# Gate and up projections in token-major form, and a Fourier token transform that sums in four pair banks

## The chip, the cores and the metric

The kernel runs on one core of a Trainium2 chip. The metric is the device time of one execution in microseconds (us), from the kernel's start to its end; the lower the better.

## What is computed

Two transformer blocks on 256 tokens of width 1024, in float32. The parts that matter here:

```
ff = silu(h @ w_gate) * (h @ w_up) @ w_down          # hidden width 2816, three times in all
f  = fftn(h.reshape(B, S, 4, 256), axes=(1, 3), norm="ortho").real
m  = f.reshape(B, S, 1024) @ w_fourier_out           # the Fourier mixer, once
x  = x + g1 * m;  h = modulate(rmsnorm(x), shift, scale)
```

The feed-forward network (FFN) stands in the first block and in both layers of the second. The mixer is a transform over the 256 features of each of four groups ("feature transform") and then over the 256 tokens ("token transform"), both done as matmuls with a table of cosines and sines, `cs`.

## The kernel before

**Split operands.** Each float32 operand is held as a high part (rounded to the format fp32r) and a low part (the rest), and every product is three matmuls: low times high, high times high, high times low (`passes`, L402). All weights come through one stream of 1 MB chunks into three slots of `raw` (SyncE, L336 to L338). A chunk w becomes `w_hi` by a copy on ScalarE (L757) and `w_lo` by a subtraction on VectorE (L1125), in a ring of four (WS = 4): `tick(w)` on both engines splits chunk w + 4, and waits for TensorE to be through with chunk w. Some chunks ("ada") aren't split: VectorE multiplies them with a row and sums them (L1134). All engines work through orders written out by hand.

**Two forms of a projection.** In token-major form (`wide`, L420 to L439) the 128 tokens of a tile are the stationary operand and 512 columns of weights stream: 24 matmuls of 512 columns for each 1 MB chunk. In feature-major form (`feat`, L441) 128 columns of weights are stationary and 256 tokens stream: 48 matmuls of 256 columns a chunk. Both read the same bytes and stream the same number of columns. The first leaves tokens on partitions and the second leaves features on partitions, as the next product needs them.

**FFN** (`ffn`, L528, L845, L1237). The hidden width is worked in 11 groups of 256 (GROUPS), two chunks each, and each group's gate and up halves land in one of the two `pair` buffers (two PSUM banks each). ScalarE takes silu of the gate half into `prod` (L855), VectorE multiplies by the up half (L1243). Groups 0 and 1 (WIDE = 2) are token-major, so their `prod` is transposed on TensorE (`turn`, L499 to L504: four transposes into a bank of `tp`) before it is split into `gt_hi` and `gt_lo` (L775, L1191). Groups 2 to 10 are feature-major: ScalarE and VectorE split `prod` directly (L861, L1249). Then `down` (L546) multiplies `gt` by 11 chunks (`outer`, L468 to L494).

**Fourier mixer** (L652 to L689 on TensorE, L1017 to L1050 on ScalarE, L1511 to L1540 on VectorE). The gate projection `pleg` fills pair 0 with token tile 0 and pair 1 with tile 1. For each tile VectorE and ScalarE update `xres`, take its norm and write `xn`; TensorE transposes that (jobs `norm2`, `norm2b`), and VectorE and ScalarE scale and split it into `ht`. Then the feature transform of that tile follows, four jobs of six 512-column matmuls in the two `tp` banks (L668), each split into `tt` (L775, L1191). After both tiles the token transform runs: four jobs of 24 matmuls of 256 columns in the `tp` banks (L682), each split into `ht` (jobs `dft2`), and then `fo`, four chunks (L687). The four matmuls of `gate_rows` (L525) and two copies (L889) stand between the two tiles. A job k in `tp` claims its bank, i.e. waits until job k - 2 was read.

## Time and profile before

| | us |
|---|---|
| three runs: median (lowest to highest) | 1202.21 (1200.54 to 1202.5) |
| the profiled execution, its own time | 1202.72 |
| its span, first to last instruction | 1200.2 |
| TensorE busy in the span | 1154.6 |
| VectorE busy | 855.3 |
| ScalarE busy | 521.5 |

The mean granted TensorE clock was 0.988 of full speed. The busy time of TensorE counts pipelined matmuls, so it says where the engine had work in flight and not how fast it went; how fast it went is read from the starts of matmuls, or from a stretch divided by the matmuls in it. The rows below give starts in us from the span's start.

### The profile page before, as it was taken

The page shows a single profiled execution, that of the slowest core. Times are in us where ns is not written, and L with a number is a line of the kernel's source. Part 1 is how long each engine was busy: PE and PEld are TensorE (multiplying, and loading weights), DVE is VectorE, ACT ScalarE, POOL GpSimd, SP SyncE. Part 2 cuts the span into 40 slices and gives each one's busy share as a digit, 9 for nine tenths or more (in the row PEclk, how much of TensorE's full clock was granted, in tenths as well). Part 3 has the DMA queues.
Part 4 walks back from the last instruction along what each step waited for, and adds up shares of the span by engine and source line. Part 5 has one row for each costly group of instructions (what it writes and reads, how often), then busy time and mean ns, then how long its engine had stood idle before and what let it go on. Part 6 is the DMA issues. An engine that isn't in the chain of part 4 may idle for free.

```text
span 1200.2 us, 16339 instructions
## 1 busy us (share of the span) xinstructions
PE 1154.6 (96%) x7012; PEld 1023.0 (85%) x7012; DVE 855.3 (71%) x1007; ACT 521.5 (43%) x463; POOL 33.1 (3%) x53
## 2 busy tenths in 40 slices
PE   6999999999899999998999999999999999999996
PEld 5898898878699998876789998879976877999985
DVE  5689989975766677575657677478956857767755
ACT  5566555633444344444344344344322433434430
POOL 1000100000000000000000000000001000000000
PEclk8999999999999999998999999999999999999998
DMA  8763474447357768531356778548753563776761
GB/s 315 269 245 137 140 265 153 150 174 256 141 197 262 297 256 321 203 141 47 132 203 239 292 268 298 214 157 318 280 203 130 208 248 140 249 296 258 289 241 36
DMA packets 38647, 259.95 MB, mean 217 GB/s; under 512 B 4144, under 2 KB 6448, under 8 KB 7856
## 3 DMA queue, kind: packets, MB, share of 16 engines
q1 hardware_dynamic: 36960, 251.84, 57.4%
q0 software_dynamic: 1616, 7.08, 1.7%
q8 instruction: 55, 0.90, 0.3%
q14 instruction: 16, 0.13, 0.0%
HBM read 257.86 MB, written 1.05 MB: 216 GB/s over the span
## 4 chain that ended last, share of the span: by engine, by line
PE 75%; DVE 14%; DMA 4%; issue 3%; ACT 3%; POOL 1%; SPq 0%; DVEq 0%; POOLq 0%; ACTq 0%
PE pair L450 33%; PE pair L485 22%; PE pair L424 13%; DVE w_lo L1125 6%; DMA raw<-stream 3%; DVE hb L1173 2%; PE tp L568 2%; PE tp L503 1%; DMA mskf<-masks 1%; PE tp L730 1%; ACT w_hi L757 1%; PE tp L682 1%; DVE raw L1134 1%; PE tp L525 1%; POOL st L357 1%
## 5 line engine op out<-in xcount | busy, mean ns | idle before, releaser
L1125 DVE TENSOR_TENSOR w_lo<-raw,w_hi 128x2048 fp32r<-128x2048 f32 x182 | 415.3, 2289 | 104.8 <-ACT w_hi L757 104.7
L757 ACT ACTIVATE w_hi<-raw 128x2048 fp32r<-128x2048 f32 x182 | 344.5, 1911 | 212.2 <-DMA raw<-stream 125.9
L450 PE MATMUL pair<-ht_hi,w_lo 128*128 128x256 f32 x1184 | 336.1, 284 | 0.9 <-DVE w_lo L1125 0.9
L450 PE MATMUL pair<-ht_lo,w_hi 128*128 128x256 f32 x1184 | 335.0, 283 | 0.0
L450 PE MATMUL pair<-ht_hi,w_hi 128*128 128x256 f32 x1184 | 335.0, 283 | 0.0
L450 PEld LDWEIGHTS pair<-ht_hi,w_lo 128*128 128x128 f32 x1184 | 227.2, 192 | 1.2 <-DVE w_lo L1125 1.1
L450 PEld LDWEIGHTS pair<-ht_hi,w_hi 128*128 128x128 f32 x1184 | 227.2, 192 | 0.1
L450 PEld LDWEIGHTS pair<-ht_lo,w_hi 128*128 128x128 f32 x1184 | 227.2, 192 | 0.0
L424 PE MATMUL pair<-w_hi,ht_lo 128*128 128x512 f32 x384 | 156.3, 407 | 20.8 <-DVE w_lo L1125 12.3
L424 PE MATMUL pair<-w_lo,ht_hi 128*128 128x512 f32 x384 | 150.7, 392 | 0.0
L424 PE MATMUL pair<-w_hi,ht_hi 128*128 128x512 f32 x384 | 150.7, 392 | 0.0
L485 PE MATMUL pair<-w_hi,gt_lo 128*128 128x512 f32 x360 | 142.5, 396 | 2.6 <-DVE gt_lo L1191 1.6
L485 PE MATMUL pair<-w_lo,gt_hi 128*128 128x512 f32 x360 | 140.7, 391 | 0.0
L485 PE MATMUL pair<-w_hi,gt_hi 128*128 128x512 f32 x360 | 140.6, 391 | 0.0
L1134 DVE SCALAR_TENSOR_TENSOR raw<-raw,crow 128x1024 f32<-128x1024 f32 x112 | 132.4, 1220 | 0.6 <-DMA raw<-stream 0.5
L424 PEld LDWEIGHTS pair<-w_hi,ht_lo 128*128 128x128 f32 x384 | 72.8, 190 | 41.4 <-issue 14.6
L1243 DVE TENSOR_TENSOR prod<-prod,pair 128x512 f32<-128x512 f32 x33 | 22.7, 688 | 107.4 <-ACT prod L855 107.4
L855 ACT ACTIVATE prod<-pair 128x512 f32<-128x512 f32 x33 | 19.8, 599 | 180.5 <-PE pair L450 159.6
L424 PEld LDWEIGHTS pair<-w_lo,ht_hi 128*128 128x128 f32 x384 | 72.6, 189 | 15.6
L424 PEld LDWEIGHTS pair<-w_hi,ht_hi 128*128 128x128 f32 x384 | 72.8, 190 | 15.1 <-issue 1.2
L485 PEld LDWEIGHTS pair<-w_hi,gt_lo 128*128 128x128 f32 x360 | 68.0, 189 | 17.4 <-DVE gt_lo L1191 1.8
L485 PEld LDWEIGHTS pair<-w_hi,gt_hi 128*128 128x128 f32 x360 | 68.0, 189 | 14.3 <-issue 0.5
(203 smaller groups left out, 1091.2 us busy)
## 6 DMA issues: line engine op xcount, KB each, us to landing
raw<-stream SPq DMA_DIRECT2D x238, 1024.0 KB, 5.0
xres<-x SPq DMA_DIRECT2D x2, 512.0 KB, 6.1
prow<-rows POOLq DMA_DIRECT2D x1, 1024.0 KB, 8.3
xres<-x POOLq DMA_DIRECT2D x2, 512.0 KB, 5.7
dt<-decay POOLq DMA_DIRECT2D x1, 1024.0 KB, 7.8
outT<-outb SPq DMA_DIRECT2D x4, 256.0 KB, 2.2
csr<-dft POOLq DMA_DIRECT2D x1, 768.0 KB, 4.6
crow<-rows POOLq DMA_DIRECT2D x1, 512.0 KB, 5.8
```

The source lines that it names most:

```text
L357: g.tensor_tensor(st[:, r, 2, 0:w], st[:, r, 1, 0:w], expo[:, 0:w], ALU.pow).then_inc(rstd_done, 1)
L424: mm = pe.matmul(pair[use % 2][:, t, :], a[:, 4 * c + k, t * P:(t + 1) * P], b[:, w % WS, k * 512:(k + 1) * 512], start=(c == 0 and k == 0 ...
L450: mm = pe.matmul(pair[use % 2][:, c, m * S:(m + 1) * S], a[:, k, m * P:(m + 1) * P], b[:, k, :], start=(k == 0 and n == 0), stop=(k == KT ...
L485: mm = pe.matmul(pair[(use + t) % 2][:, half, :], src(a, k0 + 2 * c + k, t), wsp[b][:, (w + c) % WS, k * D + half * 512:k * D + half * 512 ...
L503: mm = pe.transpose(tp[k % 2][:, n * P:(n + 1) * P], a, idn[:])
L568: mm = pe.matmul(tp[k % 2][:, hd * P:(hd + 1) * P], sk[:, hd, s * P:(s + 1) * P], sq[:, hd, s * P:(s + 1) * P], start=True, stop=True)
L757: sc.activation(w_hi[:, w % WS, :], raw[:, n % RAW, :], ACT.Copy).then_inc(hi_done, 1)
L855: sc.activation(prod[:, j % 2, :, :], pair[(use + j) % 2][:, :, 0:256], ACT.Silu).then_inc(silu_done, 1)
L1125: v.tensor_tensor(w_lo[:, w % WS, :], raw[:, n % RAW, :], whi32[:, w % WS, :], ALU.subtract).then_inc(raw_done, 1)
L1134: ins = v.scalar_tensor_tensor(out=src, in0=src, scalar=1.0, in1=crow[:], op0=ALU.mult, op1=ALU.mult, accum_out=mod[:, 2 * a + half:2 * a ...
L1173: ins = v.tensor_scalar(dst(k, half)[:, m * P:(m + 1) * P], tp[k % 2][:, m * P:(m + 1) * P], scale[:, f:f + 1], None if shift is None else ...
L1243: v.tensor_tensor(prod[:, j % 2, :, :], prod[:, j % 2, :, :], pair[(use + j) % 2][:, :, 256:512], ALU.mult).then_inc(evac[(use + j) % 2], 1)
```

## The change

The rest of the FFN's groups become token-major: `feat` calls go, every group is `wide`, and the transposes of group j - 1 are issued behind the matmuls of group j; those of group 10 are issued behind the first chunk of `down`. The direct splits from `prod` go (their semaphores `hid_hi`, `hid_done` too), and all 11 groups are split from `tp`. The host packs all gate and up weights in chunks of 512 columns. WIDE and PEELED are gone; FIRST = 2 is the first group behind the head.

In the mixer the token transform sums into the four banks of the two pairs (`mixed(gr)`), one bank a group. Each token tile adds its 12 matmuls a group: tile 0's ahead of tile 1's feature transform, groups 0 and 1 ahead of tile 1's transposes and groups 2 and 3 behind them. `gate_rows` moves behind that. The transposes of tile 0 of `norm2` move from behind the second to behind the third step of `pleg`'s second half. On ScalarE and VectorE the splits of fo's chunks 1 and 2 (`tick(w - 2)`, `tick(w - 1)`) move ahead of the splits of tile 1's feature transform and of the token transform. The transforms' results are split from the pair banks, and `fo` starts when groups 0 and 1 are split.

```diff
-             ("h0", WIDE, "split"), ("tx", 4, "split"),
+             ("h0", GROUPS, "split"), ("tx", 4, "split"),
              ("norm2", 2, "norm"), ("dft1", 4, "split"),
-             ("rows0", 2, "row_copied"), ("norm2b", 2, "norm"), ("dft1b", 4, "split"), ("dft2", 4, "split"),
-             ("norm3", 4, "norm"), ("h1", WIDE, "split"), ("rows1", 2, "row_copied"),
+             ("norm2b", 2, "norm"), ("rows0", 2, "row_copied"), ("dft1b", 4, "split"),
+             ("norm3", 4, "norm"), ("h1", GROUPS, "split"), ("rows1", 2, "row_copied"),
              ("norm4", 4, "norm"), ("sc", 4, "sc_read"), ("rows2", 2, "row_copied"),
              ("av", 8, "av_read"), ("ty", 8, "split"), ("norm5", 4, "norm"),
-             ("h2", WIDE, "split"), ("rows3", 2, "row_copied"), ("norm6", 4, "fin_read")]
+             ("h2", GROUPS, "split"), ("rows3", 2, "row_copied"), ("norm6", 4, "fin_read")]
...
+        def mixed(gr):
+
+            return pair[(USE["fo"] + gr // 2) % 2][:, gr % 2, :]
...
+            def hidden(name, jobs, j):
+
+                wait_evac(pe, USE[name] + j)
+                turn(JOB[jobs] + j, [prod[:, j % 2, t, m * P:(m + 1) * P] for m in range(2) for t in range(TT)])
+
             def ffn(name, jobs, norm, split):
 
-
-                w, use, k = W0[name], USE[name], JOB[jobs]
-
-                def hidden(j):
-                    wait_evac(pe, use + j)
-                    turn(k + j, [prod[:, j % 2, t, m * P:(m + 1) * P] for m in range(2) for t in range(TT)])
-
-                turned_head(w, use, norm, split)
-                hidden(0)
-                for c in range(2):
-                    feat(w + 4 + c, use + 2, c)
-                hidden(1)
-                for j in range(PEELED, GROUPS):
-                    for c in range(2):
-                        feat(w + 2 * j + c, use + j, c)
+                turned_head(W0[name], USE[name], norm, split)
+                hidden(name, jobs, 0)
+                for j in range(FIRST, GROUPS):
+                    wide(W0[name] + 2 * j, USE[name] + j)
+                    hidden(name, jobs, j - 1)
 
             def down(name, jobs, after):
 
-                n = GROUPS - WIDE
-                wait_split(jobs, WIDE)
-                pe.wait_ge(hid_done, n * int(name[-1]) + n - 1)
                 outer(W0[name], GROUPS, USE[name], tiles(gt),
-                      before={(GROUPS - 1, 0): lambda: pe.wait_ge(hid_done, n * int(name[-1]) + n)},
-                      after=after)
+                      before={(0, 0): lambda: wait_split(jobs, GROUPS - 2),
+                              (GROUPS - 2, 0): lambda: wait_split(jobs, GROUPS - 1),
+                              (GROUPS - 1, 0): lambda: wait_split(jobs, GROUPS)},
+                      after={(0, 1): lambda: hidden(name.replace("down", "ffn"), jobs, GROUPS - 1), **after})
...
                   after={(1, 0): turn_tile("tx", xres, 1, x_ready, 4),
-                         (1, 1): turn_tile("norm2", xn, 0, xn_done, 5)})
+                         (2, 1): turn_tile("norm2", xn, 0, xn_done, 5)})
 
             wait_split("norm2", 2)
             pe.wait_ge(cs_done, 1)
-            for t in range(TT):
+            def features(name, t):
+
                 for gr in range(4):
-                    k = JOB["dft1b" if t else "dft1"] + gr
+                    k = JOB[name] + gr
                     claim(k)
                     for d in range(2):
                         for n, (a, b) in enumerate(passes(ht, cs)):
                             mm = pe.matmul(tp[k % 2][:], a[:, 2 * gr + d, t * P:(t + 1) * P], b[:, d, 0:512],
                                            start=(d == 0 and n == 0), stop=(d == 1 and n == 2))
                     mm.then_inc(tp_done, 1)
-                if t == 0:
-                    gate_rows("rows0", 1)
-                    turn_tile("norm2", xn, 1, xn_done, 6)()
-                    wait_split("norm2b", 2)
-            for gr in range(4):
-                wait_split("dft1b", gr + 1)
-                k = JOB["dft2"] + gr
-                claim(k)
-                for m in range(2):
-                    for n, (t, part) in enumerate([(0, 0), (0, 1), (1, 0), (1, 1)]):
-                        for o, (a, b) in enumerate(passes(tt, cs)):
-                            mm = pe.matmul(tp[k % 2][:, m * S:(m + 1) * S],
-                                           a[:, t, gr, part * S + m * P:part * S + (m + 1) * P],
-                                           b[:, t, 2 * part * S:(2 * part + 1) * S],
-                                           start=(n == 0 and o == 0), stop=(n == 3 and o == 2))
-                mm.then_inc(tp_done, 1)
+
+            def tokens(name, t, groups):
+
+                for gr in groups:
+                    wait_split(name, gr + 1)
+                    for m in range(2):
+                        for part in range(2):
+                            for o, (a, b) in enumerate(passes(tt, cs)):
+                                mm = pe.matmul(mixed(gr)[:, m * S:(m + 1) * S],
+                                               a[:, t, gr, part * S + m * P:part * S + (m + 1) * P],
+                                               b[:, t, 2 * part * S:(2 * part + 1) * S],
+                                               start=(t == 0 and m == 0 and part == 0 and o == 0),
+                                               stop=(t == 1 and m == 1 and part == 1 and o == 2))
+                    if t:
+                        mm.then_inc(mix_done, 1)
+
+            features("dft1", 0)
+            wait_evac(pe, USE["pleg"])
+            wait_evac(pe, USE["pleg"] + 1)
+            tokens("dft1", 0, (0, 1))
+            turn_tile("norm2", xn, 1, xn_done, 6)()
+            tokens("dft1", 0, (2, 3))
+            gate_rows("rows0", 1)
+            wait_split("norm2b", 2)
+            features("dft1b", 1)
+            tokens("dft1b", 1, range(4))
             outer(W0["fo"], 4, USE["fo"], tiles(ht),
-                  before={(c, 0): lambda c=c: wait_split("dft2", c + 1) for c in range(4)},
+                  before={(c, 0): lambda c=c: pe.wait_ge(mix_lo, max(c + 1, 2)) for c in range(4)},
                   after={(1, 1): turn_tile("norm3", xn, 0, xn_done, 7)})
...
+            def hidden_his(jobs, j):
+
+                k = JOB[jobs] + j
+                hi(k, gt[0][:, 2 * j:2 * j + 2, :], _two(tp[k % 2][:], k))
+
             def ffn(name, jobs):
-                w, use, k, n0 = W0[name], USE[name], JOB[jobs], (GROUPS - WIDE) * int(name[-1])
-
-                def gate(j):
-
+                w, use = W0[name], USE[name]
+                for j in range(GROUPS):
                     pair_ready(w + 2 * j + 1)
-                    if j == WIDE:
-                        act.wait_ge(tp_done, k + 1)
-                    elif j > WIDE:
-                        at_least(act, hid_done, n0 + j - WIDE)
+                    if j >= 2:
+                        act.wait_ge(tp_done, JOB[jobs] + j - 1)
                     sc.activation(prod[:, j % 2, :, :], pair[(use + j) % 2][:, :, 0:256], ACT.Silu).then_inc(silu_done, 1)
...
-                for j in range(PEELED, GROUPS):
-                    gate(j)
-                    hidden_hi(j)
+                        hidden_his(jobs, j - 1)
                     tick(w + 2 * j)
                     tick(w + 2 * j + 1)
...
                 if t:
                     dft_his("dft1", 0, (2, 3))
-                    gate_rows("rows0", grow[0])
                 norm_his("norm2", t)
                 if t == 0:
                     tick(w - 3)
+            gate_rows("rows0", grow[0])
+            tick(w - 2)
             dft_his("dft1b", 1, range(4))
+            tick(w - 1)
             for gr in range(4):
-                k = JOB["dft2"] + gr
-                hi(k, ht[0][:, 2 * gr:2 * gr + 2, :], _two(tp[k % 2][:], k))
-                if gr != 2:
-                    tick(w - 2 + (gr + 1) // 2)
+                act.wait_ge(mix_done, gr + 1)
+                sc.activation(ht[0][:, 2 * gr:2 * gr + 2, :], mixed(gr).rearrange("p (a b) -> p a b", a=2),
+                              ACT.Copy).then_inc(mix_hi, 1)
+            tick(w)
...
+            def hidden_los(jobs, j):
+
+                k = JOB[jobs] + j
+                lo(k, gt[1][:, 2 * j:2 * j + 2, :], gt32[:, 2 * j:2 * j + 2, :], tp[k % 2][:].rearrange("p (a b) -> p a b", a=2))
+
             def ffn(name, jobs):
-                w, use, k, n0 = W0[name], USE[name], JOB[jobs], int(name[-1])
-
-                def gate(j):
-
-                    at_least(dve, silu_done, GROUPS * n0 + j + 1)
+                w, use = W0[name], USE[name]
+                for j in range(GROUPS):
+                    dve.wait_ge(silu_done, GROUPS * int(name[-1]) + j + 1)
...
-                        turned_lo(0)
+                        hidden_los(jobs, j - 1)
+                    if j >= FIRST:
+                        ada(ADA_AT[w + 2 * j - 1])
...
+            tick(w - 2)
             dft_los("dft1b", 1, range(4))
+            tick(w - 1)
             for gr in range(4):
-                k = JOB["dft2"] + gr
-                lo(k, ht[1][:, 2 * gr:2 * gr + 2, :], ht32[:, 2 * gr:2 * gr + 2, :], tp[k % 2][:].rearrange("p (a b) -> p a b", a=2))
-                if gr != 2:
-                    tick(w - 2 + (gr + 1) // 2)
+                dve.wait_ge(mix_hi, gr + 1)
+                v.tensor_tensor(ht[1][:, 2 * gr:2 * gr + 2, :], mixed(gr).rearrange("p (a b) -> p a b", a=2),
+                                ht32[:, 2 * gr:2 * gr + 2, :], ALU.subtract).then_inc(mix_lo, 1)
+            tick(w)
...
-        m, out = 256 * WIDE, []
-        for a, b, n in ((wg[:, :m], wu[:, :m], 256), (wg[:, m:], wu[:, m:], 128)):
-            c = np.stack([a.reshape(D, -1, n), b.reshape(D, -1, n)], axis=2).reshape(D, -1)
-            out.append(deep(c, 2 * n))
-        return np.concatenate(out)
+        return deep(np.stack([wg.reshape(D, -1, 256), wu.reshape(D, -1, 256)], axis=2).reshape(D, -1), 512)
```

## Rows read from the trace of the kernel before

**Rows 1.** The page: busy time of TensorE; the chain by line

```profile
PE 1154.6 (96%) x7012; PEld 1023.0 (85%) x7012; DVE 855.3 (71%) x1007; ACT 521.5 (43%) x463; POOL 33.1 (3%) x53
PE pair L450 33%; PE pair L485 22%; PE pair L424 13%; DVE w_lo L1125 6%; DMA raw<-stream 3%; DVE hb L1173 2%; PE tp L568 2%; PE tp L503 1%; DMA mskf<-masks 1%; PE tp L730 1%; ACT w_hi L757 1%; PE tp L682 1%; DVE raw L1134 1%; PE tp L525 1%; POOL st L357 1%
```

**Rows 2.** Chain in order of time (start, us, what): groups 3 to 10 of ffn0

```profile
350.63 92.15 PE pair L450 x768
```

**Rows 3.** Windows: two token-major chunks (rvb), the head of rva (busy, clock, DMA)

```profile
857.18:868.09 10.91, 10.91 (x49) 9.02 (x49) 10.84 (x17) 3.85 (x2) 0.00 (x0) 1.00 0.70 275
799.91:811.11 11.20, 11.20 (x50) 9.28 (x51) 4.84 (x3) 4.75 (x3) 0.00 (x0) 1.00 0.26 89
```

**Rows 4.** Timeline of TensorE: eight transposes between token-major matmuls (rg)

```profile
940.62 0.40 PE L424 MATMUL pair<-w_lo,ht_hi 128*128 128x512 f32 x1
940.85 1.04 PE L503 MATMUL tp<-idn,gg 128*128 128x128 f32 x8
941.65 0.48 PE L424 MATMUL pair<-w_hi,ht_lo 128*128 128x512 f32 x1
941.97 0.39 PE L424 MATMUL pair<-w_hi,ht_hi 128*128 128x512 f32 x1
```

**Rows 5.** Timeline of ScalarE and VectorE: one group of ffn0, and its end

```profile
431.29 0.60 ACT L855 ACTIVATE prod<-pair 128x512 f32<-128x512 f32 x1 [5.92 <-PE pair L450]
433.18 3.70 ACT L757 ACTIVATE w_hi<-raw 128x2048 fp32r<-128x2048 f32 x2
...
431.92 0.69 DVE L1243 TENSOR_TENSOR prod<-prod,pair 128x512 f32<-128x512 f32 x1 [3.23 <-ACT prod L855]
432.52 1.22 DVE L1134 SCALAR_TENSOR_TENSOR raw<-raw,crow 128x1024 f32<-128x1024 f32 x1
...
437.93 2.28 DVE L1125 TENSOR_TENSOR w_lo<-raw,w_hi 128x2048 fp32r<-128x2048 f32 x1
```

**Rows 6.** The page's DMA issues: KB each, us from issue to landing

```profile
raw<-stream SPq DMA_DIRECT2D x238, 1024.0 KB, 5.0
```

**Rows 7.** Timeline of TensorE in the mixer, and the token transform in the chain

```profile
527.25 1.09 PE L503 MATMUL tp<-idn,xn 128*128 128x128 f32 x8 [1.01 <-DVE xn L1162]
...
537.30 0.50 PE L668 MATMUL tp<-cs_hi,ht_lo 128*128 128x512 f32 x1 [0.77 <-DVE tt_lo L1191]
...
541.91 1.96 PE L525 MATMUL tp<-dg,ones 128*128 128x512 f32 x4 [1.23 <-DVE tt_lo L1191]
543.79 1.42 PE L503 MATMUL tp<-idn,xn 128*128 128x128 f32 x8
...
548.61 0.79 PE L668 MATMUL tp<-cs_hi,ht_lo 128*128 128x512 f32 x1 [3.40 <-DVE ht_lo L1185]
...
557.02 11.55 PE tp L682 x96
```

**Rows 8.** Timeline of ScalarE and VectorE in the mixer

```profile
531.16 1.90 ACT L757 ACTIVATE w_hi<-raw 128x2048 fp32r<-128x2048 f32 x1
...
533.09 2.29 DVE L1125 TENSOR_TENSOR w_lo<-raw,w_hi 128x2048 fp32r<-128x2048 f32 x1 [1.05 <-ACT w_hi L757]
535.30 1.22 DVE L1522 TENSOR_TENSOR xn<-xn,gsig 128x1024 f32<-128x1024 f32 x1
536.55 0.69 DVE L1191 TENSOR_TENSOR tt_lo<-tp,tt_hi 128x512 fp32r<-128x512 f32 x1
...
540.41 0.75 DVE L1162 TENSOR_SCALAR xn<-xres,st 128x1024 f32<-128x1024 f32 x1 [0.66 <-POOL st L357]
...
547.87 0.69 DVE L1185 TENSOR_TENSOR ht_lo<-hb,ht_hi 128x512 fp32r<-128x512 f32 x1 [0.17 <-ACT ht_hi L775]
```

**Rows 9.** Windows (busy PE, PEld, DVE, ACT, POOL; then granted clock, DMA share, GB/s)

```profile
310.00:312.00 2.00, 0.00 (x0) 0.00 (x0) 2.00 (x1) 1.93 (x3) 0.00 (x0) 1.00 0.00 0
546.00:548.00 2.00, 0.00 (x0) 0.00 (x0) 1.83 (x6) 1.12 (x2) 0.00 (x0) 0.70 0.00 0
552.00:554.00 2.00, 2.00 (x6) 1.55 (x6) 0.69 (x1) 0.20 (x2) 0.00 (x0) 0.59 0.00 0
```

More of the change, by code:

```diff
@@ L53 @@
     NW += _n
-WIDE = 2
-PEELED = 3
+FIRST = 2
 NADA = 56
 def ffn_adas(name):
-    return [W0[name] + 2 * j - 1 for j in range(WIDE, GROUPS)]
+    return [W0[name] + 2 * j - 1 for j in range(FIRST, GROUPS)]
 ADA_TICKS = [0, 1, 2, 5, 17, 18, 20, 31, 33]
@@ L284, in program @@
         consts = sem("consts")
-        hid_hi = sem("hid_hi")
-        hid_done = sem("hid_done")
         zg_done = sem("zg_done")
@@ L309, in program @@
         rot_done = sem("rot_done")
+        mix_done = sem("mix_done")
+        mix_hi = sem("mix_hi")
+        mix_lo = sem("mix_lo")
         y_done = sem("y_done")
@@ L996, in _ @@
                 if c == 0:
+                    hidden_his("h0", GROUPS - 1)
                     act.wait_ge(p_in, 16)
@@ L1055, in _ @@
                 tick(w)
+                if w == W0["down1"]:
+                    hidden_his("h1", GROUPS - 1)
             boundary(W0["down1"] + GROUPS - 1, RQ["norm4"], "norm4", 9)
@@ L1098, in _ @@
                 tick(w)
+                if w == W0["down2"]:
+                    hidden_his("h2", GROUPS - 1)
             for t in range(TT):
@@ L1235, in gate_diagonals @@
                 ins.then_inc(dg_done, 1)
+            def hidden_los(jobs, j):
+                k = JOB[jobs] + j
+                lo(k, gt[1][:, 2 * j:2 * j + 2, :], gt32[:, 2 * j:2 * j + 2, :], tp[k % 2][:].rearrange("p (a b) -> p a b", a=2))
             def ffn(name, jobs):
-                w, use, k, n0 = W0[name], USE[name], JOB[jobs], int(name[-1])
-                def gate(j):
-                    at_least(dve, silu_done, GROUPS * n0 + j + 1)
+                w, use = W0[name], USE[name]
+                for j in range(GROUPS):
+                    dve.wait_ge(silu_done, GROUPS * int(name[-1]) + j + 1)
                     v.tensor_tensor(prod[:, j % 2, :, :], prod[:, j % 2, :, :], pair[(use + j) % 2][:, :, 256:512],
                                     ALU.mult).then_inc(evac[(use + j) % 2], 1)
-                def hidden_lo(j):
-                    where = slice(2 * j, 2 * j + 2)
-                    at_least(dve, hid_hi, (GROUPS - WIDE) * n0 + j - WIDE + 1)
-                    v.tensor_tensor(gt[1][:, where, :], prod[:, j % 2, :, :], gt32[:, where, :],
-                                    ALU.subtract).then_inc(hid_done, 1)
-                def turned_lo(j):
-                    lo(k + j, gt[1][:, 2 * j:2 * j + 2, :], gt32[:, 2 * j:2 * j + 2, :],
-                       tp[(k + j) % 2][:].rearrange("p (a b) -> p a b", a=2))
-                for j in range(WIDE):
-                    gate(j)
                     if j:
-                        turned_lo(0)
+                        hidden_los(jobs, j - 1)
+                    if j >= FIRST:
+                        ada(ADA_AT[w + 2 * j - 1])
                     tick(w + 2 * j)
-                    tick(w + 2 * j + 1)
-                for j in range(WIDE, PEELED):
-                    gate(j)
-                    ada(ADA_AT[w + 2 * j - 1])
-                    tick(w + 2 * j)
-                    hidden_lo(j)
-                    turned_lo(1)
-                    tick(w + 2 * j + 1)
-                for j in range(PEELED, GROUPS):
-                    gate(j)
-                    ada(ADA_AT[w + 2 * j - 1])
-                    tick(w + 2 * j)
-                    hidden_lo(j)
                     tick(w + 2 * j + 1)
@@ L1495, in _ @@
                 if c == 0:
+                    hidden_los("h0", GROUPS - 1)
                     mod_columns(0, 24, 18)
@@ L1563, in _ @@
                 if w == W0["down1"]:
+                    hidden_los("h1", GROUPS - 1)
                     mod_columns(40, 48, 30)
@@ L1650, in _ @@
             tick(W0["down2"])
+            hidden_los("h2", GROUPS - 1)
             mod_columns(88, 96, 53)
```

15 lines of the change are left out of this document (removed).

## The prediction

> **What bounds the kernel now.** I read the page first: TensorE is busy 96% of the span, and two thirds of the chain that ended last are matmuls of projections; L450, the feature-major form, alone has 33% [rows 1]. The chain in order of time then shows that through an FFN nothing but TensorE counts: groups 3 to 10 of ffn0 stand in it as one piece, 768 matmuls in 92.15 us, and the same piece of 92.15 comes back in ffn1 and ffn2 [rows 2]. So in the FFN a change is worth what it does to the rate of matmuls. In the mixer it is otherwise: TensorE sits idle for VectorE and ScalarE [rows 7]. So there a change is worth what it puts into those gaps, less what it puts in front of the engines that end them.
>
> **FFN: the price of a group.** Before, a group is 96 matmuls of 256 columns: 92.15 / 8 = 11.52 us, 120.0 ns each [rows 2]. After, it is 48 of 512 columns. The cleanest stretch of that form is the two chunks of rvb: 48 matmuls in 10.91 us, 227.3 ns each, with VectorE busy 10.84 of them, so it isn't a rate of a quiet moment [rows 3]. A token-major group saves 0.61. It pays for four transposes. Between the matmul ahead of eight of them (940.62) and the second one behind them (941.97) lie 1.35 us where two steps of 0.227 would lie without them: 0.90 for eight, of which 0.09 is the slow first step behind them; the transposes follow each other at 0.11 ((1.04 - 0.27 of tail) / 7), so four cost 0.90 - 4 x 0.11 = 0.46 [rows 4]. A group then takes 11.37 and saves 0.15. Nine groups change in each of three FFNs, 27 in all: 27 x 0.15 = **4.0 us**. Groups 0 and 1 are token-major and transposed already.
>
> The bounds of that term: if the refill of 0.09 didn't come, 27 x 0.24 = 6.5 saved. The other end is the head of rva, whose 48 matmuls and two more stretch over 11.20 with granted clock 1.00 [rows 3]; at that rate a group would be 11.20 + 0.46, and 27 x 0.14 = 3.8 lost. I take the 10.91, because that row has two chunks in a row behind others, as groups 2 to 10 have; the head is the first work behind a norm.
>
> **FFN: the other engines.** None becomes the bound. Say a group's matmuls end at T (431.25 in the rows). ScalarE's silu runs T to T + 0.6 and VectorE's product to T + 1.4 [rows 5]. The four transposes of the group before end at T + 0.46, so ScalarE's copy from `tp` follows the silu at once, where it used to wait for the product: w_hi starts at about T + 1.2 and not at T + 1.9 (433.18). VectorE does the low part (0.69) ahead of the ada chunk (two of 1.22) and two w_lo (2.29 each); it did one of 0.68 between the two w_lo. Its sum stays, and its last w_lo ends at T + 9.0 as before (437.93 + 2.28 = 440.2) [rows 5]; the first ends 0.7 later, at T + 6.8, and its chunk is wanted at T + 11.4. The stream: three chunks in 11.37 and not 11.52, and a slot comes free 2.7 before the T at which w_hi soon wants the chunk; a landing takes 5.0 [rows 6], so the second w_hi may start some tenths late, still 4 us ahead of need. SyncE issues the same loads in the same order, and POOL is passed by nothing. The new wait (silu of group j for the transposes of j - 2) is met a whole group earlier. Behind the last group, `down`'s first chunk (2.7) covers the product of group 10 (1.4), and the splits of groups 9 and 10 are wanted seven chunks later. I cost these waits and copies at nothing; what hides them is those 11.37 us of matmuls, and without that cover a copy would cost 0.6 and a subtraction 0.69.
>
> **Mixer: the clockwork.** In the order of the code, by durations of the rows:
> - TensorE waited 1.01 for `xn` of tile 0. Now it does its third step first, 12 x 0.227 = 2.7, so the transposes start at 526.24 + 2.7 = 528.9 and not 527.25: 1.6 later [rows 7]. Queued behind them on VectorE and ScalarE are the split of tile 0, the split of fo's chunk 0 and then tile 1's sum. So w_hi goes from 531.2 to 532.8, w_lo to 534.7, the product of L1522 to 536.9, the third feature job on TensorE from 537.30 to 538.9, and `xn` of tile 1 from 540.4 to 542.0 [rows 7, 8]. This part by itself loses 1.6.
> - The feature transform of tile 0 ends at 542.1. Then groups 0 and 1 of the token transform: 96 matmuls took 11.55, 0.12 each, so 24 take 2.9 [rows 7]: 545.0. `xn` was there at 542.8, so the transposes of tile 1 start at 545.0 and not 543.79: 1.2 late in all.
> - Its `ht_lo` ends 1.2 later, 547.87 + 0.69 + 1.2 = 549.8 [rows 8]. Meanwhile TensorE does the transposes (0.9), groups 2 and 3 (2.9) and the gate rows (1.9 from 541.91 to 543.79): 550.7. The 3.40 that it waited at 548.61 is filled [rows 7]. Instead of 548.6, tile 1's feature transform starts at 550.7, with half of the token transform behind it: 5.8 of work done for 2.1 of delay.
> - New on the way: `tick(w - 2)` stands ahead of tile 1's splits. ScalarE copies the second gate row to 551.4, then w_hi to 553.3; VectorE w_lo to 555.6, then the first low part to 556.2. TensorE has done two feature jobs by 553.5 and the third has to have the bank of the first: it waits 2.7. It used to wait little there. The last two jobs end at 559.0, the second half of the token transform (48 matmuls, 5.8) at 564.8.
> - `tick(w - 1)` keeps VectorE to 563.8, then the low parts of groups 0 and 1 end at 565.1. `fo` starts at 565.2. Before it started at 557.02 + 11.55 = 568.6 [rows 7]. I count **3.3 us**. Behind it all waits are as before, only earlier.
>
> What it costs is the clock's to decide too. The granted clock fell to half once TensorE had done only gate rows and transposes and then nothing (0.70 between 546 and 548), and was back only near 553.6 (0.59 between 552 and 554), so the matmuls from 548.6 ran at half rate for 5 us, about 2.4 us lost; a stretch of 2 us with no matmul at 310 did not bring it down [rows 9]. In the new order matmuls stand on both sides of the transposes. My two waits, 2.5 (536.4 to 538.9) and 2.7 (553.5 to 556.2), are of the kind that left it up; if one brings it down, about 2.3 us are lost. The term's ends are 0 (the clock falls, 2.3, and the late `xn` costs one more) and 5 (no wait of 2.7, of which one is then spent at `fo` on its chunks' splits).
>
> **The sum.** 4.0 + 3.3 = 7.3 us, off the profiled execution's 1202.7 (span 1200.2): 1195.4. The median of the runs stands 0.5 below that execution: **1194.9 us**, 0.6% faster.
>
> **A page against the trace.** The rows say 120.0 ns for 256 columns and 227.3 for 512: each matmul carries some 13 ns on top of its columns, which is what halving their number wins back [rows 2, 3]. The Trainium skill (TensorE: Matmul & The Clock Gate, Back-to-back issue gap) puts this at N / 2.4 + 2.5 ns, 262 and 518 cycles, that is 109 and 216 ns. By that rule a group would be 10.48 before and 10.36 + 0.46 after, an FFN change of 27 x 0.34 = 9 us slower, an estimate from that page; the trace disagrees at both sizes, and more at 256. I go by the rows.
>
> **The rivals.**
> - *Slower: in the FFN the matmuls go by columns alone.* Both forms stream the same columns, so if the 13 ns weren't a matter of count but of this stage (its weights freshly split, its ring at work), the groups would keep 11.52 and the transposes come on top: 27 x 0.46 = 12.4, less 3.3: 9.1 slower, 1211. It decides from 233 ns a matmul: (11.52 - 0.46) / 48 = 230 for the FFN by itself, 233 with the mixer's 3.3 against it. For it: the head's 11.20 / 48 = 233 [rows 3]. Against it: 227.3 in rvb with the same ring. 4%. The rule of the Trainium skill quoted above (Back-to-back issue gap) points the same way.
> - *The clock falls in the mixer* in one of the two waits: the mixer gives 1.0, the whole 5.0: 1197.2. 17%.
> - *The mixer gives nothing*, because the splits of fo's chunks that moved ahead hold up more than I count (a raw chunk that isn't there, a bank claimed late) and the late `xn` comes through: 4.0 alone, 1198.2. 9%.
> - *The group stays at its 11.52*, the transposes just eating the gain: 3.3 alone, 1198.9. 6%. Between this and the first lies a change that can't be told from none.
>
> **How the numbers follow.** The forecast has 64%. The cases above are on the side of less gain, so the range goes from 1192.3 (the refill free for half the groups, the mixer 1 better) to 1198.6, which takes in the second and third rival. Over 0.2% (2.4 us, what a measurement here can tell from none) faster: forecast, clock, mixer and half-gain cases, 91%; within it 5%; slower 4%.
>
> **What the changed profile should show.** L450 gone from the FFNs; pieces of about 11.37 us a group at L424 with four transposes of `prod` between, and no wait of TensorE there; spacing of 227 ns in the FFN. In the mixer the transposes of tile 0 0.3 later than before (1.6 later, and 1.35 earlier by ffn0); a wait of TensorE of about 2.7 on `tt_lo` in tile 1's feature transform; the token transform in two halves of 5.8; granted clock 1.00 throughout; `fo` 3.3 closer to the end of `pleg`. A spacing over 230 ns in the FFN, waits of TensorE on w_lo there, or a clock of 0.5 in the mixer would make it wrong.

## The result, and the profile after

The changed kernel takes **1193.51 us** (median of 4 runs, 1192.2 to 1194.04); the kernel before took 1202.26 beside it. The ratio is 0.9929, 95% interval 0.9916 to 0.9942: 8.75 us or 0.7% faster, where I forecast 1194.9 and 7.3 us. A second set of six runs (E3 below) gave 0.9940 (0.9925 to 0.9955). So the forecast holds; what has to be settled is whether its two terms were right, and where 1.4 us more came from.

The page of the profiled execution (1193.46 us, span 1191.1), first the engines' busy time, then the chain by line; L428 is now the token-major matmul, L489 `outer`, L454 the feature-major one:

```profile
PE 1149.2 (96%) x5824; PEld 965.9 (81%) x5824; DVE 852.7 (72%) x1007; ACT 521.0 (44%) x463; POOL 33.0 (3%) x53
PE pair L428 38%; PE pair L489 25%; PE pair L454 7%; DVE w_lo L1122 6%; PE tp L507 2%; DMA raw<-stream 2%; PE tp L566 2%; DVE hb L1170 2%; DMA mskf<-masks 1%; PE tp L739 1%; ACT w_hi L766 1%; PE tp L593 1%; PE tp L529 1%; PE tp L717 1%; DVE at L1326 1%
```

Against [rows 1] TensorE has 1188 matmuls fewer and about the same busy time: busy time wouldn't have shown the gain. The feature-major share of the chain fell from 33% to 7%, and the token-major one rose from 13% to 38%.

The chain in order of time (start, us, what), two groups of ffn0, the mixer from the third feature job of tile 0 on, and `fo`:

```profile
336.86 10.93 PE pair L428 x48
348.23 10.92 PE pair L428 x48
...
537.38 1.66 PE tp L667 x6
539.04 2.86 PE pair L678 x24
542.78 2.87 PE pair L678 x24
545.65 1.73 PE tp L529 x4
547.90 1.92 ACT w_hi L766
549.84 2.29 DVE w_lo L1122
552.79 4.37 PE tp L667 x12
557.68 1.92 ACT w_hi L766
559.62 2.29 DVE w_lo L1122
561.91 1.21 DVE ht_lo L1516 x2
563.16 16.63 PE pair L489 x72
```

A group starts 348.23 - 336.86 = 11.37 us behind the one before it, 11.52 in [rows 2]. A piece of the chain begins at the modelled end of what stands before it. By starts of instructions, a group's 48 matmuls take 347.63 - 336.62 = 11.01 us, its first slow step included, and the transposes the other 0.36:

```profile
336.26 0.60 PE L507 MATMUL tp<-idn,prod 128*128 128x128 f32 x4
336.62 0.48 PE L428 MATMUL pair<-w_hi,ht_lo 128*128 128x512 f32 x1
347.63 0.60 PE L507 MATMUL tp<-idn,prod 128*128 128x128 f32 x4
```

In the mixer the chain is the one of the prediction: tile 0's token matmuls, gate rows, then the split of fo's chunk 1 on ScalarE and VectorE, on which the third feature job waits, then the split of chunk 2, and `fo`.

Stages, in us. A stage runs between starts of ScalarE's instructions: the silu of each group (`prod<-pair`) and the first sigmoid of `pleg` (`gsig<-pair`), and the first matmul of `fo`. E3 and E4 are second profiles of the two kernels:

| stage | before | E4, before again | changed | E3, changed again |
|---|---|---|---|---|
| start to first silu of ffn0 | 332.84 | 333.39 | 331.02 | 332.30 |
| ffn0, silu 2 to silu 11 | 104.53 | 104.53 | 102.28 | 102.26 |
| to the first sigmoid of pleg | 78.02 | 77.98 | 78.95 | 78.98 |
| sigmoid to `fo` | 47.57 | 47.61 | 45.47 | 44.12 |
| `fo` to first silu of ffn1 | 43.82 | 43.85 | 43.95 | 43.91 |
| ffn1, silu 2 to silu 11 | 104.53 | 104.54 | 102.28 | 102.28 |
| to first silu of ffn2 (retention) | 293.71 | 293.89 | 293.30 | 293.23 |
| ffn2, silu 2 to silu 11 | 104.53 | 104.53 | 102.28 | 102.28 |
| to the end | 74.28 | 74.28 | 75.23 | 75.23 |

An FFN's nine groups take 2.25 less. But before, two sets of transposes lay between these silus and now nine do; those of groups 9 and 10 lie behind the last silu and show as 0.93 to 0.95 more in each following stage. Net: 3 x 2.25 - (0.93 + 0.93 + 0.95) = **3.9 us**. The mixer gives 2.1 in the first profile and 3.5 in the second. That leaves 1.8 us ahead of the first FFN and 293.71 - 293.30 + 0.93 = 1.3 in the retention layer between ffn1 and ffn2. The program is the same in both places.

In steady state ScalarE and VectorE run through a group so (rows of the timeline; the matmuls of the silu's group ended at about 427.34):

```profile
427.37 0.60 ACT L865 ACTIVATE prod<-pair 128x512 f32<-128x512 f32 x1 [4.71 <-PE pair L428]
427.86 0.59 ACT L784 ACTIVATE gt_hi<-tp 128x512 fp32r<-128x512 f32 x1
428.34 1.92 ACT L766 ACTIVATE w_hi<-raw 128x2048 fp32r<-128x2048 f32 x1
430.74 1.92 ACT L766 ACTIVATE w_hi<-raw 128x2048 fp32r<-128x2048 f32 x1 [0.48 <-DMA raw<-stream]
...
428.00 0.69 DVE L1243 TENSOR_TENSOR prod<-prod,pair 128x512 f32<-128x512 f32 x1 [3.02 <-ACT prod L865]
428.61 0.69 DVE L1188 TENSOR_TENSOR gt_lo<-tp,gt_hi 128x512 fp32r<-128x512 f32 x1
...
431.49 4.49 DVE L1122 TENSOR_TENSOR w_lo<-raw,w_hi 128x2048 fp32r<-128x2048 f32 x2
```

Compared with [rows 5], ScalarE copies the hidden part at once behind the silu and reaches w_hi 1.0 after the group's end and not 1.9. It then outruns the stream and waits 0.48 for the second chunk. VectorE is through 8.6 us after the group's end, 2.7 before the next group's.

### The profile page after: what moved, and what is told of

It is laid out like the page before. It is cut to its first block, busy times and chain, and to the rows that moved or that the text cites. A ratio compares the mean times of both kernels' runs of the same rounds, so it can differ in the third digit from the quotient of the medians.

```text
span 1191.1 us, 13987 instructions
## 1 busy us (share of the span) xinstructions
PE 1149.2 (96%) x5824; PEld 965.9 (81%) x5824; DVE 852.7 (72%) x1007; ACT 521.0 (44%) x463; POOL 33.0 (3%) x53
## 4 chain that ended last, share of the span: by engine, by line
PE 77%; DVE 13%; issue 4%; DMA 3%; ACT 2%; POOL 1%; SPq 0%; DVEq 0%; POOLq 0%; ACTq 0%
PE pair L428 38%; PE pair L489 25%; PE pair L454 7%; DVE w_lo L1122 6%; PE tp L507 2%; DMA raw<-stream 2%; PE tp L566 2%; DVE hb L1170 2%; DMA mskf<-masks 1%; PE tp L739 1%; ACT w_hi L766 1%; PE tp L593 1%; PE tp L529 1%; PE tp L717 1%; DVE at L1326 1%
## 5 line engine op out<-in xcount | busy, mean ns | idle before, releaser
L428 PE MATMUL pair<-w_hi,ht_lo 128*128 128x512 f32 x816 | 327.5, 401 | 19.5 <-DVE w_lo L1122 10.9
L428 PE MATMUL pair<-w_lo,ht_hi 128*128 128x512 f32 x816 | 319.3, 391 | 0.0
L428 PE MATMUL pair<-w_hi,ht_hi 128*128 128x512 f32 x816 | 319.2, 391 | 0.0
L428 PEld LDWEIGHTS pair<-w_hi,ht_lo 128*128 128x128 f32 x816 | 154.1, 189 | 56.2 <-issue 14.7
L428 PEld LDWEIGHTS pair<-w_lo,ht_hi 128*128 128x128 f32 x816 | 153.9, 189 | 32.9
L428 PEld LDWEIGHTS pair<-w_hi,ht_hi 128*128 128x128 f32 x816 | 154.3, 189 | 31.2 <-issue 1.2
L489 PE MATMUL pair<-w_hi,gt_lo 128*128 128x512 f32 x360 | 142.3, 395 | 1.6 <-DVE gt_lo L1188 1.6
L489 PE MATMUL pair<-w_lo,gt_hi 128*128 128x512 f32 x360 | 140.3, 390 | 0.0
L489 PE MATMUL pair<-w_hi,gt_hi 128*128 128x512 f32 x360 | 140.1, 389 | 0.0
L454 PE MATMUL pair<-ht_hi,w_lo 128*128 128x256 f32 x320 | 91.1, 285 | 0.5 <-DVE w_lo L1122 0.5
L454 PE MATMUL pair<-ht_lo,w_hi 128*128 128x256 f32 x320 | 90.5, 283 | 0.0
L454 PE MATMUL pair<-ht_hi,w_hi 128*128 128x256 f32 x320 | 90.5, 283 | 0.0
L489 PEld LDWEIGHTS pair<-w_hi,gt_lo 128*128 128x128 f32 x360 | 67.6, 188 | 15.8 <-DVE gt_lo L1188 1.8
L489 PEld LDWEIGHTS pair<-w_hi,gt_hi 128*128 128x128 f32 x360 | 67.6, 188 | 14.1 <-issue 0.5
L489 PEld LDWEIGHTS pair<-w_lo,gt_hi 128*128 128x128 f32 x360 | 67.6, 188 | 14.2
L454 PEld LDWEIGHTS pair<-ht_hi,w_lo 128*128 128x128 f32 x320 | 61.4, 192 | 0.9 <-DVE w_lo L1122 0.7
L454 PEld LDWEIGHTS pair<-ht_hi,w_hi 128*128 128x128 f32 x320 | 61.4, 192 | 0.1
```

What stands on the lines that cost most here:

```text
L428: mm = pe.matmul(pair[use % 2][:, t, :], a[:, 4 * c + k, t * P:(t + 1) * P], b[:, w % WS, k * 512:(k + 1) * 512], start=(c == 0 and k == 0 ...
L454: mm = pe.matmul(pair[use % 2][:, c, m * S:(m + 1) * S], a[:, k, m * P:(m + 1) * P], b[:, k, :], start=(k == 0 and n == 0), stop=(k == KT ...
L489: mm = pe.matmul(pair[(use + t) % 2][:, half, :], src(a, k0 + 2 * c + k, t), wsp[b][:, (w + c) % WS, k * D + half * 512:k * D + half * 512 ...
```

## The experiments

**Parts and repeats.** E1 has the changed kernel's FFN and the mixer of before, E2 the reverse, E3 and E4 are the two kernels again. Of the edits of E1 and E2, which take the whole mixer, these lines mark the order of TensorE:

```diff
 E1: changed kernel, mixer of before
-            tokens("dft1", 0, (0, 1))
-            turn_tile("norm2", xn, 1, xn_done, 6)()
-            tokens("dft1", 0, (2, 3))
...
 E2: kernel before, mixer of the changed one
+            tokens("dft1", 0, (0, 1))
+            turn_tile("norm2", xn, 1, xn_done, 6)()
+            tokens("dft1", 0, (2, 3))
```

> The FFN part alone; mixer, its order and its banks as before. By my sum: 27 groups x 0.15 us = 4.0 us less than the kernel before (about 1198.2, ratio 0.9967), groups of 11.37 us. By the rival that matmuls go by columns alone in the FFN: 27 x 0.46 = 12 us more. By the rival that the parts of the kernel that weren't touched got faster with the change in the FFN (fewer instructions, other code loading): 7 us less or more, with the head before the first FFN 1.8 us shorter here too.

> The mixer part alone; FFNs as before. By my sum 3.3 us less with the clock up (ratio 0.9973), 2.0 to 2.2 us less where the clock falls in the 2.5 us wait ahead of the third feature job of tile 1, as it did in the profile of the changed kernel; the stretch from the first sigmoid of the gate projection to the first matmul of fo 45.5 us (clock low) or 44.3 (clock up) and not 47.6. By the rival that the untouched parts got faster with this part: 5 us less or more.

> The changed kernel once more, for a second profile and a narrower interval. If the 3.2 us by which untouched stretches (before the first FFN 1.8, retention 1.3) were shorter in its first profile are chance of that one execution (the clock in the first 20 us and ahead of the first FFN, a landing of 7.4 us in the kernel before), those stretches come out elsewhere in a second profile, by 1 us or more, and the ratio is near 0.9940. If they come with the change, they repeat within 0.3 us and the ratio is 0.993 or less.

> The kernel before, unchanged, for a second profile. If the untouched stretches vary by chance, its time up to the first FFN's first silu (332.8 in the first profile) or its stretch through retention (293.7) differs by 1 us or more from its first profile; if not, both repeat within 0.3 us and stand above those of the changed kernel by 1.8 and 1.3.

E1: 1195.55 us, ratio 0.9951 (0.9938 to 0.9964). Its FFN stages are those of the changed kernel to 0.02 us. My 0.9967 lies just outside that interval: against the median of before beside it (1201.7) it is 6.2 us and not 4.0, and between the two profiles more still. The stages say where that is: 1.9 ahead of the first FFN (330.95), 1.3 in retention (293.30, with 0.93 of moved transposes), and 0.7 in a mixer whose code is that of before (46.85; the clock was low for a shorter time there). E2: 1197.79 us, ratio 0.9969 (0.9957 to 0.9981), mixer 45.38, retention 293.71 as before, start 331.52. The two ratios multiplied give 0.9920. That lies within the interval of the first set for the whole, and just outside that of E3, which ran beside them (0.9925 to 0.9955). So the medians alone don't show that the parts add; the stages do: E1 has the FFN stages of the changed kernel, and E2 its mixer (45.38 beside 45.47, the clock falling once in both).

E3 and E4 part the rest. The start came out at 332.30 where it had been 331.02, and over all profiles of this study it lies between 330.95 and 334.03 with no order by kind of kernel. So that term is chance of the execution. Retention repeated in these four, 293.7 to 293.9 with the old FFN and 293.2 to 293.3 with the new, so chance alone doesn't explain it; E9 and E10 below take it up. The mixer of the changed kernel came out 1.35 shorter in E3. The windows (busy PE, PEld, DVE, ACT, POOL, then granted clock) show why; first the changed kernel's first profile, then E3:

```profile
550.00:552.00 2.00, 0.28 (x2) 0.00 (x0) 2.00 (x1) 0.89 (x2) 0.00 (x0) 1.00 0.00 0
552.00:554.00 2.00, 1.21 (x3) 1.02 (x4) 1.33 (x3) 0.00 (x0) 0.00 (x0) 0.57 0.35 66
554.00:556.00 2.00, 2.00 (x7) 1.57 (x6) 0.00 (x0) 0.25 (x1) 0.00 (x0) 0.58 0.96 406
```

```profile
550.00:552.00 2.00, 1.59 (x7) 0.95 (x6) 0.85 (x1) 1.97 (x3) 0.00 (x0) 1.00 0.03 8
552.00:554.00 2.00, 0.00 (x0) 0.00 (x0) 2.00 (x3) 0.23 (x1) 0.00 (x0) 1.00 0.00 0
554.00:556.00 2.00, 1.91 (x8) 1.61 (x9) 0.64 (x2) 0.22 (x1) 0.00 (x0) 1.00 0.75 201
```

Both have the same wait of 2.50 us, from 550.29 to 552.79 in the first and from 551.59 to 554.09 in the second. In the first the clock fell to half at the end of the wait, and the matmuls after it ran at half rate until near 555.7; in the second it stayed up.

**The price of a group.** E5 does each 512-column matmul of groups 2 to 10 as two of 256 columns in the same token-major form. E6 issues each group's transposes twice.

```diff
 E5, in wide_part; split is 2 for groups 2 to 10
-                        mm = pe.matmul(pair[use % 2][:, t, :], a[:, 4 * c + k, t * P:(t + 1) * P],
-                                       b[:, w % WS, k * 512:(k + 1) * 512],
...
+                        for half in range(split):
+                            m = 512 // split
+                            mm = pe.matmul(pair[use % 2][:, t, half * m:half * m + m], a[:, 4 * c + k, t * P:(t + 1) * P],
+                                           b[:, w % WS, k * 512 + half * m:k * 512 + half * m + m],
...
 E6, in hidden
+                for again in range(2):
+                    for n, (m, t) in enumerate([(m, t) for m in range(2) for t in range(TT)]):
+                        mm = pe.transpose(tp[k % 2][:, n * P:(n + 1) * P], prod[:, j % 2, t, m * P:(m + 1) * P], idn[:])
```

> The changed kernel, but in groups 2 to 10 of each FFN every 512-column matmul is done as two of 256 columns on the same token tile: token-major form, 96 matmuls a group. If the 0.61 us that a group wins comes from the number of matmuls, they take 120 ns each, a group is 11.52 + 0.46 = 11.98 us, and the nine groups take 5.5 us more than in the changed kernel (102.3), 107.8. If it comes from the form (which operand is stationary), the spacing of 256 columns is 113.7 ns and the nine stay at 102.3.

> The changed kernel with each group's four transposes of prod issued twice into the same bank. If transposes cost TensorE their 0.11 us each and nothing hides them, the nine groups take 9 x 0.44 = 4.0 us more (106.3), the whole 33 x 0.44 = 14.5 us more. If they slip in beside weight loads or waits, less than half of that.

E5: the nine groups took 107.57, 5.29 more than the 102.28 of the changed kernel, at 1212.41 us for the whole (one run). Two of its groups in the chain in order of time:

```profile
351.82 11.52 PE pair L430 x96
363.78 11.52 PE pair L430 x96
```

Those are the 11.52 us of the feature-major groups, 120.0 ns a matmul, in token-major form. So what a group wins is won by halving the number of matmuls, and not by the form: (11.52 - 10.92) / 48 = 12.5 ns for each one saved. Each matmul of E5 has a weight load of its own, even where both halves use the same weights; whether the 12.5 ns belong to the matmul or to its load no run here tells. E6: the nine groups took 106.10, 3.82 more, 0.42 for four transposes, and the whole 1207.05 us (one run). Transposes are paid in full. A group's own four cost 11.37 - 10.92 = 0.45, so 0.03 comes once a set, where I had counted 0.09 for the slow first step behind them.

**The mixer's two delays.** E7 puts tile 0's transposes back behind the second step of `pleg`; E8 moves the split of fo's chunk 1 behind the first two feature splits of tile 1, on both engines; E11 has both; E12 also splits fo's chunk 2 behind the first two groups of the token transform.

```diff
 E7, E11, E12
-                         (2, 1): turn_tile("norm2", xn, 0, xn_done, 5)})
+                         (1, 1): turn_tile("norm2", xn, 0, xn_done, 5)})
...
 E8, E11, E12: ScalarE, and VectorE with dft_los
-            tick(w - 2)
-            dft_his("dft1b", 1, range(4))
+            dft_his("dft1b", 1, range(2))
+            tick(w - 2)
+            dft_his("dft1b", 1, range(2, 4))
...
 E12: ScalarE, and VectorE alike
-            tick(w - 1)
             for gr in range(4):
+                if gr == 2:
+                    tick(w - 1)
                 act.wait_ge(mix_done, gr + 1)
```

> The changed kernel with the transposes of tile 0 of norm2 back behind the second step of the gate projection. By my step on them (1.6 us of delay that goes through to fo), the stretch from the first sigmoid to fo is 1.6 us shorter than in the changed kernel: 43.9 with the clock low for one fall, 42.5 with it up. By the rival that the 1.0 us wait of TensorE for xn comes back and eats it: 0.6 us shorter or less.

> The changed kernel with the split of fo's chunk 1 moved behind the splits of groups 0 and 1 of tile 1's feature transform, on ScalarE and VectorE. By my theory that this split alone makes TensorE wait 2.5 us at the third feature job (and lets the clock fall): that wait goes, the clock stays up there, and fo starts 2.8 us earlier than in the first profile of the changed kernel (stretch from 45.5 to about 42.7), 1.4 earlier than with the clock up. By the rival that the wait only moves behind the second two groups' splits: the stretch stays within 0.5 of 44.1.

> The changed kernel with the transposes of tile 0 back behind the second step and the split of fo's chunk 1 behind the first two feature splits of tile 1. If the two terms add: 1.6 and 1.4 to 2.8 off the stretch from the first sigmoid to fo, i.e. 41.1 with the clock up and about 42 with one fall; the kernel about 1191 and ratio 0.991. If the waits are the same one counted twice: 42.5 or more.

> As the one before, and the split of fo's chunk 2 moved behind the splits of groups 0 and 1 of the token transform. On VectorE 2.3 us of that split stood between the end of the token transform and fo's start; by that, fo starts up to 2 us earlier than in the one before (stretch about 40 with the clock up), if TensorE isn't held up by the token matmuls themselves: they end about when the split does, so the gain is 0.3 to 1. By the rival that fo then waits for its chunk 2 or 3: no shorter than the one before, and a wait for w_lo inside fo.

| kernel | median us | ratio (95%) | sigmoid to `fo` | waits of TensorE at the feature jobs |
|---|---|---|---|---|
| changed (E3) | 1193.62 | 0.9940 (0.9925 to 0.9955) | 44.12 | 1.03, 2.18, 2.50 |
| E7 | 1195.04 | 0.9926 (0.9903 to 0.9949) | 44.17, clock low behind the 2.50 | 0.77, 2.50 |
| E8 | 1192.46 | 0.9915 (0.9896 to 0.9933) | 43.21, clock low behind the 2.18 | 1.02, 2.18 |
| E11 | 1190.11 | 0.9901 (0.9887 to 0.9915) | 40.54 | 0.77 |
| E12 | 1190.25 | 0.9906 (0.9893 to 0.9919) | 39.79 | 0.76 |

The waits come from the timeline of TensorE; of E3, E8 and E12 it has these rows, with the idle time and its releaser at the end:

```profile
531.76 0.50 PE L667 MATMUL tp<-cs_hi,ht_lo 128*128 128x512 f32 x1 [1.03 <-DVE ht_lo L1182]
536.95 0.50 PE L667 MATMUL tp<-cs_hi,ht_lo 128*128 128x512 f32 x1 [2.18 <-DVE tt_lo L1188]
554.09 0.50 PE L667 MATMUL tp<-cs_hi,ht_lo 128*128 128x512 f32 x1 [2.50 <-DVE tt_lo L1188]
```

```profile
532.08 0.50 PE L667 MATMUL tp<-cs_hi,ht_lo 128*128 128x512 f32 x1 [1.02 <-DVE ht_lo L1183]
537.27 0.50 PE L667 MATMUL tp<-cs_hi,ht_lo 128*128 128x512 f32 x1 [2.18 <-DVE tt_lo L1189]
```

```profile
526.50 1.09 PE L507 MATMUL tp<-idn,xn 128*128 128x128 f32 x8 [1.01 <-DVE xn L1161]
536.55 0.50 PE L667 MATMUL tp<-cs_hi,ht_lo 128*128 128x512 f32 x1 [0.76 <-DVE tt_lo L1190]
```

In E8 the 2.50 is gone. The clock didn't stay up as I had forecast (42.7): it fell behind the wait of 2.18. Compared like with like, each with one fall, the stage went from 45.47 to 43.21, 2.26 us where I had expected 1.4. E7's median says nothing by itself, its interval is 0.5% wide; its stage does: 44.17 against 45.47, both with one fall of the clock, is 1.3 us, near my 1.6. The two add: 1.30 + 2.26 = 3.56, and E11 has 44.12 - 40.54 = 3.58, with the clock up both times. My 1.4 for the split was too small, not the rule that they add. In E8 and E11 a short wait stands at `fo`; this is E11's:

```profile
559.82 0.50 PE L489 MATMUL pair<-w_hi,ht_lo 128*128 128x512 f32 x1 [0.58 <-DVE ht_lo L1518]
```

E12 has no wait there, and its order takes 0.75 more off the stage, as expected (0.3 to 1); I can't tell its time from E11's. Its chain shows the mixer without a splitting engine in it from the gate rows to `fo`:

```profile
546.57 1.72 PE tp L529 x4
548.28 2.92 PE tp L667 x12
551.25 3.04 PE tp L667 x12
554.29 5.75 PE pair L678 x48
560.04 16.35 PE pair L489 x72
```

Both beat the changed kernel and the one before: 1190.1 and 1190.3 us, ratios of 0.9901 and 0.9906, about 1% less than before. Each group of runs has its own runs of the kernel before beside it, so between groups the ratios and stages compare, not the times.

**Retention's 1.3 us.** `ro` is the output projection of the retention layer, eight chunks, right behind the transposes of its tile `gg`. In both profiles of before TensorE waits in `ro` for a w_lo whose raw chunk landed late (1.03 and 1.22 us; chain: 7.38 us of DMA in the first, then w_hi and w_lo); in the changed kernel it doesn't. I suspected the loads of TensorE's code, 16 KB each (0.90 MB / 55). A matmul has a weight load beside it, so 7012 matmuls are 14,024 instructions before, and 5824 are 11,648 now: 255 and 253 for each load of code. With fewer instructions each load falls elsewhere. The row of the queue (packets, MB, share), of before and of the changed kernel:

```profile
q8 instruction: 55, 0.90, 0.3%
```

```profile
q8 instruction: 46, 0.75, 0.2%
```

```diff
 E9: changed kernel, behind the first transposes
+            for n in range(9):
+                pe.matmul(warm[:, 384:512], ones[:], ones[:], start=(n == 0), stop=(n == 9 - 1))
...
 E10: kernel before
-WARM = 18
+WARM = 9
```

> The changed kernel with nine more warm-up matmuls (36 TensorE instructions) in TensorE's idle time before the first weights. In the three profiles with the old FFNs a 16 KB instruction load falls 17.3 to 18.5 us behind the last transpose of gg, and the weights of the last chunk but some of ro are copied at 22.3 to 22.5; in all of the changed FFN it falls at 21.2 to 21.6 and they are copied at 19.3 to 20.1. By the theory that this load in the way of the stream costs retention its 1.3 us: 36 instructions put it 4 us earlier, at about 17.3, TensorE waits some 1 us for w_lo in ro again and the stretch from ffn1 to ffn2 goes from 293.3 to 294.6. By the rival that the place of the load doesn't matter (another cause, or chance): it stays at 293.3.

> The kernel before with nine instead of eighteen warm-up matmuls, i.e. 36 TensorE instructions fewer. By the same theory the instruction load moves from 17.3 to about 21.4 us behind the last transpose of gg, TensorE's wait for w_lo in ro (1.0 to 1.2 in both profiles of before) goes, and the stretch from ffn1 to ffn2 falls from 293.7 to 293.9 down to 292.4. By the rival it stays. The time up to the first FFN may move by 1 or 2 us either way with the clock.

Times below are from the start of the last eight transposes of `gg`. E10 did what the theory says in `ro`: the code load moved to 21.6 us, the wait went, and retention fell from 293.7 to 292.29. E9 did not: the code load moved to 18.0, retention stayed at 293.28, no wait. And E11 and E12, with the code load at 20.9 and 22.3, have a wait again, though a short one (0.23 and 0.28; retention 293.79 and 293.89). The chain in order of time through `ro`, of the kernel before, E10, the changed kernel and E12:

```profile
980.11 8.47 PE pair L485 x36
```

```profile
956.29 32.68 PE pair L485 x144
```

```profile
948.13 32.66 PE pair L489 x144
```

```profile
969.50 8.50 PE pair L489 x36
```

One piece of 144 matmuls is an `ro` without a wait; a last piece of 36 is what stands behind one. So the code load alone does not decide there. That a code load can hold up the stream is likely from another place in E10. Its time as a whole didn't fall (1202.99 us, one run), because the stretch from ffn0's last silu to `pleg` grew by 1.0, from 77.98 and 78.02 to 79.01. There the moved code load fell between the issues of two weight chunks (499.36 and 502.08), which took 6.13 and 5.94 us to land. In the other thirteen profiles no code load falls there, and the same two chunks take 4.6 to 5.2. From E10's chain and TensorE's timeline:

```profile
499.36 6.13 DMA raw<-stream
510.20 0.50 PE L485 MATMUL pair<-w_hi,ht_lo 128*128 128x512 f32 x1 [0.68 <-DVE ht_lo L1191]
```

What all profiles share in `ro` is that this chunk's copy starts 19.3 to 22.5 us behind those transposes, and TensorE waits where it starts later than 21.2: `ro` runs at the edge of what the stream brings. All ten profiles with the new FFNs are on the better side of it or close to it: eight have no wait, E11 and E12 one of at most 0.28, and even these two keep some 0.8 of the 1.3 us (293.71 + 0.93 less their 293.79 and 293.89). Of the four with the old FFNs three wait 1.03 to 1.22, and the fourth is E10. So the gain goes with the change, as a side effect and not by any step of its own; what decides it stays open.

## Why the prediction was right, and where its size was off

*The FFN term*, 27 x 0.15 = 4.0 us, measured 3.9. The step is right in each of its parts: 11.52 by E5 even for the other form, 10.92 for 48 matmuls (10.91 forecast), 0.45 for a group's four transposes (0.46 forecast) and 0.42 for four more (E6). The choice that mattered was the row of rvb and not the head of rva. The head was misread as a slower rate: its 11.20 holds the modelled end of its last matmuls. By starts the head of ffn0 in the changed kernel takes 336.26 - 325.23 = 11.03 us, and the group behind it 11.01. So the bound of 3.8 us lost, and the 233 ns that spoke for the first rival, rested on no slower matmul. The cover named for the copies and splits held: TensorE never waited in an FFN behind its head, and w_hi came some tenths late for its second chunk (0.48) as said.

*The mixer term*, 3.3 us, measured 3.5 with the clock up (E3) and 2.1 with it low (first profile). The clockwork came out step by step: delay of tile 0's transposes 1.6 (E7 takes 1.3 back), waits of 2.18 and 2.50 where I had 2.5 and 2.7. The step that was too hopeful is that such waits "are of the kind that left the clock up": of eight profiles with one or both, six show a fall of the clock in the mixer. So my second rival, at 17%, was the commoner course, and by my own signs ("granted clock 1.00 throughout") the first profile speaks against that step: its clock was low for 3.4 us, 0.57 between 552 and 554. The fall costs 1.35 and not 2.3, because the clock stayed low for less time (3.4 us where it had been 6.8 in the kernel before). That the total came out all the same owes something to luck: the stretches below, which I had at nothing, gave more than this took away.

*The sum* was 1.4 us short in the first comparison. What made it up lies in two stretches whose code the change doesn't touch: the start (1.8, chance of the execution, up to 3 us between profiles) and retention (1.3, at the edge of the stream), less the 1.2 by which the mixer of that profile fell short of its 3.3. The prediction had both stretches at nothing. The second comparison's ratio of 0.9940 is 7.2 us; its medians are 8.1 apart. My 7.3 lies within both intervals.

*The rivals.* Columns alone: refuted by the groups of 11.37 and by E5, in which 96 matmuls of 256 columns take 5.29 us more for nine groups than 48 of 512 for the same columns. The rule of the Trainium skill (TensorE: Matmul & The Clock Gate, Back-to-back issue gap) gave 109 ns and 216 ns a matmul and would have made the FFNs 9 us slower, an estimate from that page; E5's 120.0 and the changed kernel's 227.5 (10.92 / 48) are what this kernel has, so here the trace decides against it. The same section calls that rule the gap of an isolated matmul, and gives about 131 ns at 512 columns for a stream of weight load and matmul pairs. Here every matmul has a weight load, and no row comes near that either. The mixer that gives nothing and the group that stays at 11.52 are refuted by E2 and by the stages.

## What to carry to other kernels

Price a matmul by the spacing in a stretch of the same kernel, per size: here the operand of 256 columns paid 12.5 ns a matmul over the one of 512, which paid for four transposes a group and left 0.15 us. Small as that is, it comes 27 times. Where work is moved into a gap of the busiest engine, look at what else was moved with it: nearly two thirds of the further gain in the mixer (E11; 2.26 of 3.58 us) lay in a weight split that stood ahead of a split that the next matmul was waiting for, and removing such a wait also saves what a fall of the clock behind it would cost (1.35 us here). When parts of a kernel that weren't edited get faster, profile both kernels again before giving the change the credit, and look at the other stages of a run that seems to confirm a theory: E10 won 1.4 us in `ro` and lost 1.0 ahead of `pleg`.

## What the hardware showed that I had not expected

The granted clock fell at waits of TensorE of 2.18 us (E5, E8) and 2.50 us (the changed kernel, E2, E7, E9), between 0.5 us before the wait's end and 1.5 behind it, and stayed up at the same waits, with the same instructions around them, in E3 and E6. Between the two profiles of the changed kernel this place alone makes 1.35 us, and a single profile can't tell which is usual. The start of the kernel, where nothing was edited but in E9 and E10, varied by 3 us between profiles.
